# First stick-breaking head formed among the projections, causal mask added by TensorE, and a new order at both ends of the attention loop

## The reference

```python
z = jnp.einsum('bhqd,bhkd->bhqk', qb, kb).astype(jnp.float32) * scale
mask = jnp.arange(k_len)[None, :] < q_pos[:, None]
log_1m = jnp.where(mask, jax.nn.log_sigmoid(-z), 0.0)
suffix = lax.cumsum(log_1m, axis=3, reverse=True) - log_1m
a = jnp.where(mask, jnp.exp(jax.nn.log_sigmoid(z) + suffix), 0.0)
outs.append(jnp.einsum('bhqk,bhkd->bhqd', a.astype(vb.dtype), vb))
```

## Time and profile before

| | |
|---|---|
| median of three runs | 2308.8 us (2306.85 to 2310.65) |
| the profiled execution | 2308.82 us, span 2307.5 us |
| PE busy | 2258.2 us, 98% of the span |
| DVE, ACT, POOL busy | 837.0, 449.2, 1316.3 us |
| mean granted clock of PE | 0.986 |
| stretch of the projections | about 1450 to 1635 us |
| making the MLA heads | 1635 to 1671 us |
| attention loop | 1671 to 1793 us |

### The profile page before, as it was taken

The page is one execution under the profiler, slowest core; times in us unless marked ns, Lnnn a source line. Parts: engine busy times, 40 slices in busy tenths (PEclk is TensorE's granted clock), DMA queues, the critical chain, the costliest instruction groups (busy, mean ns, idle before and its releaser), DMA issues.

```text
span 2307.5 us, 25552 instructions
## 1 busy us (share of the span) xinstructions
PE 2258.2 (98%) x10762; PEld 1868.6 (81%) x10762; DVE 837.0 (36%) x930; ACT 449.2 (19%) x746; POOL 1316.3 (57%) x772
## 2 busy tenths in 40 slices
PE   8999999999999999999999999999888999999999
PEld 7888888887778888888888888878766788888887
DVE  3333204884234433203443301142557723343013
ACT  3111004323213111003111101002467121111012
POOL 5666665634145666665666665556325656666654
PEclk9999999999799999999999999999979999999999
DMA  5333322211123332332332322222200223333322
GB/s 181 101 93 99 98 94 83 74 55 55 37 82 94 99 100 92 101 93 84 98 100 92 101 93 90 92 91 93 66 1 1 91 92 92 100 95 106 101 83 91
DMA packets 55818, 200.99 MB, mean 87 GB/s; under 512 B 6680, under 2 KB 6808, under 8 KB 55576
## 3 DMA queue, kind: packets, MB, share of 16 engines
q1 hardware_dynamic: 53856, 194.14, 27.2%
q10 hardware_dynamic: 1848, 5.21, 0.6%
HBM read 197.23 MB, written 2.10 MB: 86 GB/s over the span
## 4 chain that ended last, share of the span: by engine, by line
PE 92%; DVE 4%; ACT 2%; issue 1%; POOL 0%; DMA 0%; SPq 0%; ACTq 0%; DVEq 0%
PE psum L382 19%; PE psum L383 19%; PE psum L384 19%; PE psum L463 8%; PE psum L465 8%; PE psum L464 8%; PE psum L608 1%; PE psum L958 1%; PE psum L427 1%; PE psum L663 1%; PE psum L1107 1%; PE psum L1108 1%; PE psum L1109 1%; PE psum L996 1%; PE psum L966 1%
## 5 line engine op out<-in xcount | busy, mean ns | idle before, releaser
L347 POOL TENSOR_TENSOR w_lo<-w_raw,w_hi 128x1024 fp32r<-128x1024 f32 x365 | 885.7, 2427 | 30.4
L345 POOL TENSOR_SCALAR w_hi<-w_raw 128x1024 fp32r<-128x1024 f32 x365 | 389.6, 1067 | 853.5 <-PE psum L384 597.7
L382 PE MATMUL psum<-u_hi,w_hi 128*128 128x512 f32 (+1 forms) x2072 | 794.4, 383 | 1.2 <-issue 0.8
L383 PE MATMUL psum<-u_hi,w_lo 128*128 128x512 f32 (+1 forms) x2072 | 789.0, 381 | 0.0
L384 PE MATMUL psum<-u_lo,w_hi 128*128 128x512 f32 (+1 forms) x2072 | 788.9, 381 | 0.0
L382 PEld LDWEIGHTS psum<-u_hi,w_hi 128*128 128x128 f32 x2072 | 392.5, 189 | 78.8 <-issue 4.4
L384 PEld LDWEIGHTS psum<-u_lo,w_hi 128*128 128x128 f32 x2072 | 391.8, 189 | 74.6
L383 PEld LDWEIGHTS psum<-u_hi,w_lo 128*128 128x128 f32 x2072 | 392.2, 189 | 73.6 <-issue 1.0
L463 PE MATMUL psum<-w_hi,hidden_hi 128*128 128x512 f32 x800 | 311.7, 390 | 1.0 <-DVE work L1958 1.0
L464 PE MATMUL psum<-w_lo,hidden_hi 128*128 128x512 f32 x800 | 311.2, 389 | 0.0
L465 PE MATMUL psum<-w_hi,hidden_lo 128*128 128x512 f32 x768 | 298.8, 389 | 0.0
(11 more groups left out here) (278 smaller groups left out, 1634.0 us busy)
## 6 DMA issues: line engine op xcount, KB each, us to landing
w_raw<-in_ffn_in SPq DMA_DIRECT2D x176, 512.0 KB, 3.5
w_raw<-in_ffn_out SPq DMA_DIRECT2D x88, 512.0 KB, 3.5
w_raw<-in_proj_in SPq DMA_DIRECT2D x34, 512.0 KB, 3.5
w_raw<-in_mix_in SPq DMA_DIRECT2D x29, 512.0 KB, 3.5
w_raw<-in_embed SPq DMA_DIRECT2D x10, 512.0 KB, 3.6
w_raw<-in_mix_out SPq DMA_DIRECT2D x8, 512.0 KB, 3.5
w_raw<-in_branch SPq DMA_DIRECT2D x8, 512.0 KB, 3.5
w_raw<-in_proj_out SPq DMA_DIRECT2D x8, 512.0 KB, 3.6
```

The source lines that it names most:

```text
L345: pool.tensor_scalar(hi, raw, 1.0, 1.0, ALU.mult, ALU.mult).then_inc(k.w_split, 1)
L347: pool.tensor_tensor(lo, raw, hi.bitcast(F32), ALU.subtract).then_inc(k.w_split, 1)
L382: pe.matmul(out, hi[:, cols], xhi, start=first, stop=False)
L383: pe.matmul(out, lo[:, cols], xhi, start=False, stop=False)
```

## The change

1. **Stick head 0 early.** Its logits are formed by PE after projection tile 21 (`pe_stick_logits(k, 0)`), ACT copies them and takes abs, exp and ln there (`act_stick_first`, with two table loads more), DVE ends the softplus after tile 25 (`dve_softplus(k, 0)`). They live in other buffers (`z_first`), in two pieces. The transpose of the value tiles moves from after tile 26 to after tile 27.
2. **The mask.** One bf16 matmul (128x512) now opens each head's stick logits instead of ending its suffix sums, so the logits come masked, and `dve_mask` is gone.
3. **Making the heads.** Squares go to PSUM banks 4 to 7 instead of SBUF scratch (softplus 0 lives there), and ACT copies unit u-4 out before it squares unit u, not after.
4. **Entry of the loop.** PE starts with the MLA logits of head 0, then turns the last two units, then forms the suffix sums of head 0. ACT rounds the softplus of head 0 before its last four copies.
5. **In the loop.** DVE takes the reciprocals before it forms the low part. `COMPLETE` moves the rounding of finished tiles 0, 1 and 6 an iteration later (and ACT and POOL do it there).
6. **The last head.** Its probabilities are turned into banks 0 to 2 without the wait for `z_added`; its MLA and stick values are formed together after the MLA values of head 6; the merge waits for `p_copied` 8 instead of `probs_done` 8.

```diff
+        elif i == 21:
+            pe.wait_ge(k.proj_scaled, 11)
             pe.wait_ge(k.norm_var, NORM["kl"])
             pe.wait_ge(k.kr_step, 1)
+            pe.wait_ge(k.masks_done, 3)
+            pe_stick_logits(k, 0)
+        elif i == 27:
+            pe.wait_ge(k.z_copied, 1)
             pe_turn(k, k.big[:, 14 * T:18 * T], 0, 4 * NT)
...
-        self.sq = k.sc[u % 2][:, 0:4 * self.normed]
+        self.sq = k.ps[4 + u % 4][:, 0:4 * self.normed]
...
-COMPLETE = {3: [0], 4: [4], 5: [1, 5], 6: [6], 7: [2], 8: [7, 3]}
+COMPLETE = {4: [0, 4], 5: [5], 6: [1], 7: [6, 2], 8: [7, 3]}
...
+def pe_stick_logits(k, h):
+    pe, H = k.nc.tensor, Heads(k)
+    pe.matmul(k.psum[:, A0:A0 + T], H.id16, H.nge16.unsqueeze(1).broadcast_to([P, NT, P]), start=True, stop=False, skip_group_check=True)
+    for i, t0, n, c in CAUSAL:
+        m = pe.matmul(..., start=c in (T, 2 * T), stop=True, skip_group_check=True)
+    m.then_inc(k.z_logits, 1)
...
-        m = add(0, T, H.id16, H.nge16.unsqueeze(1).broadcast_to([P, NT, P]))
...
+    logits(0)
+    for u in range(UNITS - LAG + 1, UNITS):
+        pe_turn_unit(k, u)
+    stick_sums(0)
+    stick_logits(1)
+    for h in range(1, AH):
+        if h > 1:
+            stick_logits(h)
             stick_sums(h - 1)
...
+        logits(h)
+        transpose(h - 1)
+        values(h - 1, h - 2 if h > 1 else None)
     stick_sums(AH - 1)
     transpose(AH - 1)
-    values(AH - 1, AH - 2)
-    values(None, AH - 1)
+    values(None, AH - 2)
+    values(AH - 1, AH - 1)
...
     for u in range(UNITS):
         U = Unit(k, u)
+        if u >= LAG + 1:
+            out(u - LAG - 1)
+            act.wait_ge(k.head_copied, u - LAG)
         wait_up(k, act, u)
-        if u >= 2:
-            act.wait_ge(k.head_summed, u - 1)
         act.activation(U.sq..., U.heads..., ACT.Square).then_inc(k.head_sq, 1)
...
-        if u >= LAG + 1:
-            out(u - LAG - 1)
         root(u)
+    act_soft_hi(k, 0)
...
+    split(0)
+    maxima(0)
+    divide(0)
+    for h in range(1, AH):
+        add_sums(h - 1)
         maxima(h)
-        softplus(h)
-        if h:
-            turned(h - 1)
+        dve_softplus(k, h)
+        turned(h - 1)
+        divide(h)
         split(h)
-        divide(h)
```

More of the change, by code:

```diff
@@ L1023, in values @@
                 v = H.sv[:, ((h // 2) * NT + i) * P + h % 2 * HV:((h // 2) * NT + i) * P + (h % 2 + 1) * HV]
-                z = pe.matmul(k.ps[7][half(h), t0:t0 + width], v, H.z[h % 2][:, c:c + width], start=n == 0, stop=n == last, skip_group_check=True)
+                z = pe.matmul(k.ps[7][half(h), t0:t0 + width], v, H.z_at(h, c, width), start=n == 0, stop=n == last, skip_group_check=True)
             if m is not None:
@@ L1553, in act_make_heads, with act_stick_first, act_soft_hi @@
             act.copy(U.v, U.heads[:, :, NOPE:NOPE + HV]).then_inc(k.v_copied, 1)
-        if u >= LAG + 1:
-            out(u - LAG - 1)
         root(u)
+    act_soft_hi(k, 0)
     for u in range(UNITS - LAG - 1, UNITS):
         out(u)
+def act_stick_first(k):
+    act, H = k.nc.scalar, Heads(k)
+    s = H.soft[0]
+    act.preload_act_table_set("natural_log_exp_and_others")
+    act.wait_ge(k.z_logits, 1)
+    act.wait_ge(k.lat_lo, KCQ + KCKV)
+    act.wait_ge(k.lat_summed, KCQ + KCKV)
+    act.wait_ge(k.kr_turned, 1)
+    for a, b, x in H.z_first:
+        m = act.copy(x, k.psum[:, A0 + a:A0 + b])
+    m.then_inc(k.z_copied, 1)
+    act.wait_ge(k.z_copied, 1)
+    for a, b, x in H.z_first:
+        m = act.activation(s[:, a:b], x, ACT.Abs)
+    m.then_inc(k.z_act, 1)
+    act.wait_ge(k.z_act, 1)
+    act.activation(s, s, ACT.Exp, scale=-1.0).then_inc(k.z_act, 1)
+    act.wait_ge(k.z_act, 2)
+    act.activation(s, s, ACT.Ln, bias=1.0).then_inc(k.z_act, 1)
+def act_soft_hi(k, h):
+    act, H = k.nc.scalar, Heads(k)
+    act.wait_ge(k.soft_dve, h + 1)
+    if h:
+        act.wait_ge(k.soft_summed, h)
+    else:
+        act.wait_ge(k.w_used, NUMBER["branch", 0])
+    act.copy(H.soft_hi, H.soft[h % 2]).then_inc(k.soft_hi, 1)
 def act_attend(k):
@@ L1578, in stick_logits @@
         act.activation(s, s, ACT.Exp, scale=-1.0).then_inc(k.z_act, 1)
+        act.wait_ge(k.z_act, 3 * h + 2)
+        act.activation(s, s, ACT.Ln, bias=1.0).then_inc(k.z_act, 1)
     def exponents(h):
@@ L1590, in weigh @@
     def weigh(h):
-        zh = H.z[h % 2]
         act.wait_ge(k.z_added, h + 1)
-        act.activation(zh, zh, ACT.Exp).then_inc(k.z_weights, 1)
+        for a, b, x in H.z_pieces(h):
+            m = act.activation(x, x, ACT.Exp)
+        m.then_inc(k.z_weights, 1)
     def pairs(h):
@@ L1603, in act_attend @@
     act.preload_act_table_set("natural_log_exp_and_others")
-    for h in range(AH):
-        s = H.soft[h % 2]
+    exponents(0)
+    for h in range(1, AH):
         stick_logits(h)
-        act.wait_ge(k.z_act, 3 * h + 2)
-        act.activation(s, s, ACT.Ln, bias=1.0).then_inc(k.z_act, 1)
-        if h:
-            weigh(h - 1)
+        weigh(h - 1)
         exponents(h)
-        act.wait_ge(k.soft_dve, 2 * (h + 1))
-        if h:
-            act.wait_ge(k.soft_summed, h)
-        act.copy(H.soft_hi, s).then_inc(k.soft_hi, 1)
+        act_soft_hi(k, h)
         pairs(h)
```

94 lines of the change are left out of this document (46 added, 48 removed).

## The result

The changed kernel takes 2292.6 us (median of four runs, 2290.1 to 2294.6) against 2308.9 for the kernel before in the same session: a ratio of 0.993, 95% interval 0.992 to 0.995, 16.3 us less. The forecast was 2289 with a range of 2283 to 2299.

A forecast was written before the change was run, and what follows sets the result against it. PE, busy 98% of the span, was taken to bound the kernel. Gains 12.1 + 9.6 + 1.4 less costs 2.6 and 0.8 make 19.7; 2308.8 - 19.7 = 2289.1, stated as 2289 us, range 2283 to 2299.

The forecast's parts named there:

- Entry: Entry of the loop, walked step by step from the last turns: head 1's stick logits start at 1676.6, not 1688.67; gain 12.1 us.
- If the clock stays at 1.00: Condition on the 12.1 us gain at the loop entry: PE's granted clock stays at 1.00 there, where it was 0.51.
- Loop: Head 1 to head 7: stalls in `pairs` vanish, 78.0 us becomes 6 x 11.4 = 68.4; gain 9.6 us.
- PE sets the period: In the loop, ACT's 10.9 us per head lies below the 11.4 that PE's own work fills.
- the mask costs PE nothing: In the loop, the same mask matmul only moves from the end of the sums to the head of the logits.
- rival 1: The clock falls in the loop entry all the same: 7 us lost, 2296; chance 0.20.
- Rival 2: The loop does not shorten; the two long heads stay 13.5 because DVE or ACT is late: 4.3 us, 2293; chance 0.10.
- End: From head 7's stick logits to the merge: 26.7 us becomes 24.5, less 0.8 for tile 7's low part; gain 1.4 us.
- The joint values +22.1 to +24.4: At the end, heads' joint values run from 22.1 to 24.4 us after head 7's stick logits, merge at +24.5.
- Added and making: Head 0's stick logits with mask among the projections cost 2.6 us; making the heads, with ACT's new order, costs 0.8 us.
- Rival 4: Making the heads becomes a serial line through ACT and DVE: 21 to 22 us more, 2311; chance 0.07.
- Rival 3: DVE and POOL block each other each head, the low part waiting about 1.4 us: 9.8 us, 2299; chance 0.08.

The follow-up runs named there:

- e1_values_apart: The changed kernel with the last values in the earlier order: stick head 7 with MLA head 6, then MLA head 7 alone; 2293.2 us.
- e3_divide_last: The changed kernel with DVE's reciprocal behind the low part again, as in the kernel before; 2296.9 us.
- e2_round_early: The changed kernel with the rounding of finished tiles back at the iterations of the kernel before; 2298.0 us.
- The fillers: Matmuls with results never read, laid into PE's gaps around the loop entry: 44 in the kernel before, 2299.7 us; 19 in the changed kernel, 2291.9 us.
- e9_other_half: The changed kernel with head 7's MLA values in the last joint call written to the other output half, that result left wrong; 2292.1 us.
- e4_before_filled: The kernel before with 44 matmuls of 128x512, results never read, in PE's gaps at the loop entry; 2299.7 us.
- e8_before_filled_orders: The kernel before with 44 matmuls never read, the later rounding of finished tiles, and the reciprocals ahead of the low part; 2295.0 us.

## Why the prediction was right, and where its sizes were off

The direction, the range and the order of the terms held: the entry is the largest gain, the loop next, the end small. The trace gives 14.9 where the sum said 19.7, and nearly all of the 4.8 too much lies in the first three terms.

1. **Entry, 12.1 forecast, 11.5 measured.** The walk was right in its steps: a wait for the norm (0.7 forecast, 1.05 measured), 2.6 us of logits, turns, ACT's copy and table load, four exponents. Head 1's logits came 9.1 us after the last turns, forecast 8.6. "If the clock stays at 1.00" held up to that mark in this execution, and that was luck: with the same entry the distance is 12.7 us in `e1_values_apart` and `e3_divide_last` and 10.8 in `e2_round_early`, where the clock fell earlier. The fillers divide the gain: 4.3 us of it was slow clock in the kernel before (20.7 to 16.4), 7.3 is the new order (16.4 to 9.1).
2. **Loop, 9.6 forecast, 6.1 measured, the mis-sized term.** The forecast of 11.4 for a period stood on "PE sets the period" and "the mask costs PE nothing". Both fail by a little. A period without a stall took 11.52 us before and takes 11.66 now, and what sets it is PE's logits and sums, then DVE's maxima, then ACT's exponents. The walk added up ACT alone to 10.9 us; the exponents end 11.6 us after the stick logits' start, because ACT waits 0.34 us for the maxima and its own parts take as much longer than walked. The mask costs PE 0.32 us at the head of the logits (1705.71 to 1706.03, and what taking it out gives back) where it cost 0.23 at the end of the sums, and it lies on that chain in both places. Six periods of 0.26 more: 1.6 us. The rest, 1.9, is the first period, 13.6: rival 1 in small. The clock fell not between the turns and the logits but after the gaps of the entry, at about 1685, and cost 2 us, not 7. The fillers show it: 11.57 with the clock kept. Where it fell earlier, head 2's logits came another 1.5 to 1.6 us later. Of the 6.1 us gained, 2.7 are in the first period, slow in both kernels, and 3.4 in the five others, mostly the stall. Rival 2 is refuted; the stall of `pairs` is gone and comes back with the old table.
3. **End, 1.4 forecast, 0.7 measured.** "Transposes at about +17.2" came at +17.1, but by two errors that cancel: the reciprocal came at +12.2, not +11.1 (ACT's exponents end at +11.6, and DVE is in a copy until then), and POOL took 4.62 us, not 5.7. The joint values came at +21.6, forecast 22.1. "The joint values +22.1 to +24.4" is the step that failed: 2.3 was the duration of a joint call of the loop, where the two heads are neighbours and write different halves of their banks. Heads 7 and 7 write the same half and run one after the other, 4.45 us. That costs 2.1, of which 0.5 is given back by the earlier start and 0.8 because the wait for tile 7's low part, in the sum, does not occur behind the long call.
4. **Added and making, -2.6 and -0.8 forecast, -2.7 and -0.6 measured.** The first -2.7 is the distance between two marks that scatter by 3 us (1634.72 to 1638.17 in traces of kernels alike up to there), so its fit is luck; the size itself shows in the trace, where 2.71 us pass from the mask (1566.88) to the next tile's product (1569.59). ACT's and DVE's new work among the projections cost nothing, as charged. Rival 4 is refuted: PE is busy 32.4 of the 36 us. The order of copy-out and square wasn't tried apart, since the squares now use the banks of the turned units and need the copy first; what makes the -0.6 is open.
5. **The reciprocal.** Charged at up to 0.3 us for DVE and 1.4 for POOL; measured 0.19 for DVE and 0.35 for POOL's four together (4.27 to 4.62). Rival 3 is refuted. So POOL's four end at 4.62 after their start and not at 5.7, and the reorder is worth 1.7 at the end, and more in the trace where the clock fell in the longer gap.

## What to carry to other kernels

An idle stretch of the bounding engine costs a second time where the clock falls in it: before moving work into such a stretch, lay dead matmuls into the gaps and time it. Here that cheap edit, one table of numbers and two swapped lines gave 13.7 of 16.3 us. When two series of narrow matmuls are to run side by side, look at which half of the output's partitions each one writes, and take the duration of a pair only from a pair that writes the same way. And where the bounding engine seems to have no gap left in a period, follow the chain from one start to the next through the other engines: a wait of 0.16 us hides behind a modelled end, and 0.26 us too little in the period is paid in every iteration. An experiment tells two chains apart only if its edit lies on one of them.

## What the runs showed of the hardware

- **Half-width outputs.** Two series of 14 matmuls with outputs in different halves of the partitions start within 0.04 us of each other and take 2.32 us together (`e9_other_half`), no longer than one series alone (2.38). In the same half they take turns and need 4.45. The Trainium skill (TensorEngine Tiling (Array Packing), Key Properties) says that different tiles can load and multiply in parallel; the trace of `e9_other_half` agrees. That two series in the same half can't is what the changed kernel's trace shows.
- **VectorE beside GpSimd.** A DVE product of 128x128 beside POOL's subtraction of two tensors took 2.41 us where its usual time is 0.28, and in `e9_other_half` a DVE subtraction of 512 columns beside the same POOL subtraction took 1.68 instead of 0.69. But DVE's subtraction of 1280 columns beside POOL's product with a per-partition factor took 1.68 instead of 1.49. The Trainium skill (SBUF — State Buffer, Terms) says that the loser of the shared ports fully blocks; the first two cases agree, the third does not. Which property of the third makes it nearly harmless was not tried.
- **The clock.** In the changed kernel it fell at about 1685 after gaps of 1.05, 1.11, 0.49 and 1.31 us; in `e1_values_apart`, with the same entry, between 1670 and 1671, after gaps of 0.51 and 1.05. A gap of 2.74 at the end of the kernel before went by at 1.00. After the same gap of 2.74 in `e4_before_filled` the clock was 0.50 (1776 to 1778), and after one of 2.41 in `e8_before_filled_orders` as well (1772 to 1774). The length of a gap alone does not tell whether the clock falls, so these kernels have a spread of a few us that is nobody's edit.
